# Sample attention of a hybrid decoder step: key blocks outermost over the four pairs, and a second bank for the turned probabilities

## The reference, cut to what matters

```python
s_c = jnp.einsum('bqgrd,bngd->bqgrn', qi, kc) * scale      # compressed keys
p_c = _masked_softmax(s_c, m_c, (-1,))
o_c = jnp.einsum('bqgrn,bngd->bqgrd', p_c.astype(vc.dtype), vc)
imp = ...                     # importance of each 64-key block, from p_c
_, idx = lax.top_k(score, n_top)
s_s = jnp.einsum('bqgrd,bqgksd->bqgrks', qi, k_sel) * scale   # selected blocks
p_s = _masked_softmax(s_s, m_s, (-2, -1))
o_s = jnp.einsum('bqgrks,bqgksd->bqgrd', p_s.astype(v_sel.dtype), v_sel)
s_w = jnp.einsum('bqgrd,bkgd->bqgrk', qi, k_w) * scale        # last 512 keys
p_w = _masked_softmax(s_w, m_w, (-1,))
o_w = jnp.einsum('bqgrk,bkgd->bqgrd', p_w.astype(v_w.dtype), v_w)
return gt[..., 0:1] * o_c + gt[..., 1:2] * o_s + gt[..., 2:3] * o_w
```

## Time and profile before

| | us |
|---|---|
| median of three runs (3066.73 to 3068.82) | 3068.81 |
| the profiled execution | 3069.89 |
| its span, first to last instruction | 3068.1 |
| PE busy in the span | 2789.7 (91%) |
| PE weight loads busy | 2557.5 (83%) |
| DVE busy | 1432.9 (47%) |
| ACT busy | 491.3 (16%) |
| POOL busy | 694.5 (23%) |
| mean granted clock of PE | 0.946 |

### The profile page before, as it was taken

How to read it: one execution, slowest core, us unless ns; L and a number is a source line. 1 busy time by engine, 2 the same in 40 slices (tenths; PEclk the granted TensorE clock), 3 DMA queues, 4 the chain that set the end, 5 groups by cost and what they waited for, 6 DMA issues and landing times. The chain is left out here.

```text
span 3068.1 us, 38688 instructions
## 1 busy us (share of the span) xinstructions
PE 2789.7 (91%) x15429; PEld 2557.5 (83%) x15429; DVE 1432.9 (47%) x2224; ACT 491.3 (16%) x710; POOL 694.5 (23%) x366
## 2 busy tenths in 40 slices
PE   8978786778898899999999998969899999999995
PEld 8978744445558899999999997969799999999983
DVE  4999025555643563333333335854653333333334
ACT  3011123123331220000000002031320000000002
POOL 3431002000002132233232221322133223223210
PEclk9987877699999999999999999979999999999998
DMA  4114541000003011111111111111011111111101
GB/s 152 56 34 140 122 138 41 1 1 1 1 1 114 28 42 41 41 41 45 51 42 44 45 41 28 42 35 42 21 49 41 48 41 41 48 41 41 45 10 59
DMA packets 82854, 145.01 MB, mean 47 GB/s; under 512 B 26382, under 2 KB 54286, under 8 KB 82446
## 3 DMA queue, kind: packets, MB, share of 16 engines
q1 hardware_dynamic: 60126, 129.68, 13.2%
q10 hardware_dynamic: 22640, 14.16, 1.6%
HBM read 134.88 MB, written 13.07 MB: 48 GB/s over the span
## 5 line engine op out<-in xcount | busy, mean ns | idle before, releaser
L580 PE MATMUL PS<-XH,WH 128*128 128x364 f32 x3048 | 682.5, 332 | 65.0 <-ACTq L1027 16.3
L580 PE MATMUL PS<-XL,WH 128*128 128x364 f32 x3048 | 678.5, 331 | 0.0
L580 PE MATMUL PS<-XH,WL 128*128 128x364 f32 x3048 | 678.2, 331 | 0.0
L535 POOL CAST WH<-RAW 128x1024 fp32r<-128x1024 f32 x177 | 207.4, 1172 | 2003.9 <-PE PS L580 1331.0
L580 PEld LDWEIGHTS PS<-XH,WH 128*128 128x128 f32 x3048 | 536.2, 190 | 67.9 <-issue 41.8
L580 PEld LDWEIGHTS PS<-XL,WH 128*128 128x128 f32 x3048 | 535.8, 190 | 0.0
L580 PEld LDWEIGHTS PS<-XH,WL 128*128 128x128 f32 x3048 | 535.3, 190 | 0.0
L537 POOL TENSOR_TENSOR WL<-RAW,WH 128x1024 fp32r<-128x1024 f32 x177 | 466.9, 2638 | 14.2
L561 PE MATMUL PS<-HH,WH 128*128 128x364 f32 x1056 | 354.1, 335 | 29.3 <-DVE Y L1794 15.1
L1794 DVE TENSOR_TENSOR Y<-Y,PS 128x364 f32<-128x364 f32 x480 | 254.0, 533 | 230.9 <-PE PS L566 225.9
L566 PE MATMUL PS<-HL,WH 128*128 128x364 f32 x1056 | 348.2, 330 | 0.0
(11 more groups left out here) (276 smaller groups left out, 2501.5 us busy)
## 6 DMA issues: line engine op xcount, KB each, us to landing
RAW<-wst SPq DMA_DIRECT2D x174, 512.0 KB, 3.3
KVP<-cache SPq DMA_DIRECT2D x64, 128.0 KB, 2.2
XRAW<-xT SPq DMA_DIRECT2D x8, 546.0 KB, 10.5
Y<-xT SPq DMA_DIRECT2D x8, 546.0 KB, 7.4
yT<-Y ACTq DMA_DIRECT2D x3, 1456.0 KB, 9.7
PG<-cache SPq DMA_DIRECT2D x64, 64.0 KB, 2.3
PG<-cache ACTq DMA_DIRECT2D x64, 64.0 KB, 2.3
win_old<-win_past SPq DMA_DIRECT2D x1, 4032.0 KB, 15.9
```

The source lines that it names most:

```text
L535: pool.tensor_copy(WH[:, s, :], RAW[:, s, :]).then_inc(hi_done, 1)
L580: mm = pe.matmul(PS[:, 3 * bank_set + c, 0:CH], w, x[:, k, c * CH:(c + 1) * CH], start=(q == 0 and w is hi and x is XH), stop=(q == len(ks ...
```

## The change

Four loops over the pairs are turned inside out. `L754` and `L760` get loops of their own behind those of `L753` and `L758`. `L758` runs over the halves outside and the pairs inside. `L787` and `L800` run over key blocks outside and pairs inside, with `L789` and `L802` in loops of their own behind them. `S_TURN = (6, 0)` names two banks: even turns go to bank 6, odd ones to bank 0, and PE waits before a turn only until the turn before the last has been moved. ACT's `move` reads from the bank of its turn.

```diff
--- before.py
+++ after.py
@@ -75,6 +75,7 @@
 N_W = AT_F1 + N_FFN
 POOL_ORDER = [6, 7, 4, 5, 2, 3, 0, 1]
 RING = 3
+S_TURN = (6, 0)
 CONV_STEPS = 3
 EARLY = 21
 assert N_W % RING == 0 and EARLY % RING == 0
@@ -751,12 +752,14 @@
                 pe.wait_ge(sp_loaded[b2], 18 * 16 * (gi // 2 + 1))
                 for bb, g, rows, feat, q, at in pairs():
                     pe.matmul(PS[rows, 0, :], q, KWS[b2][feat, bb, :], start=True, stop=True)
+                for bb, g, rows, feat, q, at in pairs():
                     mm = pe.matmul(PS[rows, 1, 0:SS], q, kv("kw")[feat, at:at + SS], start=True, stop=True)
                 mm.then_inc(s_win, 1)
-                for bb, g, rows, feat, q, at in pairs():
-                    for h in range(2):
+                for h in range(2):
+                    for bb, g, rows, feat, q, at in pairs():
                         pe.matmul(PS[rows, 2 + h, :], q, KVP[b2][feat, 8 * bb + 4 * h:8 * bb + 4 * h + 4, 0, :],
                                   start=True, stop=True)
+                for bb, g, rows, feat, q, at in pairs():
                     mm = pe.matmul(PS[rows, 4, 0:SS], q, kv("ks")[feat, at:at + SS], start=True, stop=True)
                 mm.then_inc(s_sel, 1)
                 pe.wait_ge(s_pc, gi + 1)
@@ -765,10 +768,10 @@
                 def turned_tiles(src, cols):
 
                     nonlocal turn
-                    if turn:
-                        pe.wait_ge(s_turned, turn)
+                    if turn >= 2:
+                        pe.wait_ge(s_turned, turn - 1)
                     for n, (lo, hi) in enumerate(cols):
-                        mm = pe.transpose(PS[0:hi - lo, 6, n * P:(n + 1) * P], src[:, lo:hi], ident)
+                        mm = pe.transpose(PS[0:hi - lo, S_TURN[turn % 2], n * P:(n + 1) * P], src[:, lo:hi], ident)
                     mm.then_inc(s_turn, 1)
                     turn += 1
 
@@ -782,10 +785,11 @@
                 turned_tiles(PB[:, 0, :], [(k * P, k * P + P) for k in range(4)])
                 turned_tiles(PB[:, 0, :], [(W_HIST, W_HIST + SS)])
                 pe.wait_ge(s_turned, turn)
-                for bb, g, rows, feat, q, at in pairs():
-                    for k in range(4):
+                for k in range(4):
+                    for bb, g, rows, feat, q, at in pairs():
                         pe.matmul(PS[rows, 7, HD:2 * HD], PTB[:, 0, k * P + 32 * (2 * bb + g):k * P + 32 * (2 * bb + g) + 32],
                                   VWS[b2][:, bb, k, feat], start=(k == 0), stop=False)
+                for bb, g, rows, feat, q, at in pairs():
                     mm = pe.matmul(PS[rows, 7, HD:2 * HD], PTB[0:SS, 0, 4 * P + 32 * (2 * bb + g):4 * P + 32 * (2 * bb + g) + 32],
                                    VN[:, 1, 2 * gi + bb, feat], start=False, stop=True)
                 mm.then_inc(s_pv, 1)
@@ -794,11 +798,13 @@
                 turned_tiles(PB[:, 1, :], [(k * P, k * P + P) for k in range(4, 8)])
                 turned_tiles(PB[:, 1, :], [(8 * P, 8 * P + SS)])
                 pe.wait_ge(s_turned, turn)
+                for k in range(8):
+                    for bb, g, rows, feat, q, at in pairs():
+                        j = 32 * (2 * bb + g)
+                        pe.matmul(PS[rows, 7, 2 * HD:3 * HD], PTB[:, k // 4, (k % 4) * P + j:(k % 4) * P + j + 32],
+                                  KVP[b2][:, 8 * bb + k, 1, feat], start=(k == 0), stop=False)
                 for bb, g, rows, feat, q, at in pairs():
                     j = 32 * (2 * bb + g)
-                    for k in range(8):
-                        pe.matmul(PS[rows, 7, 2 * HD:3 * HD], PTB[:, k // 4, (k % 4) * P + j:(k % 4) * P + j + 32],
-                                  KVP[b2][:, 8 * bb + k, 1, feat], start=(k == 0), stop=False)
                     mm = pe.matmul(PS[rows, 7, 2 * HD:3 * HD], PTB[0:SS, 0, 4 * P + j:4 * P + j + 32],
                                    VN[:, 0, 2 * gi + bb, feat], start=False, stop=True)
                 mm.then_inc(s_pv, 1)
@@ -1068,8 +1074,8 @@
                 def move(dsts):
                     nonlocal turn
                     act.wait_ge(s_turn, turn + 1)
-                    for dst, src in dsts:
-                        ins = act.activation(dst, src, ACT.Copy)
+                    for dst, rows, n in dsts:
+                        ins = act.activation(dst, PS[0:rows, S_TURN[turn % 2], 0:n], ACT.Copy)
                     ins.then_inc(s_turned, 1)
                     turn += 1
 
@@ -1081,15 +1087,15 @@
                     if kind == 0:
                         if gi:
                             act.wait_ge(s_pv, 3 * gi)
-                        move([(PTB[0:NB, 0, 0:P], PS[0:NB, 6, 0:P])])
+                        move([(PTB[0:NB, 0, 0:P], NB, P)])
                         act.wait_ge(s_pv, 3 * gi + 1)
-                        move([(PTB[:, 0, 0:4 * P], PS[:, 6, 0:4 * P])])
-                        move([(PTB[0:SS, 0, 4 * P:5 * P], PS[0:SS, 6, 0:P])])
+                        move([(PTB[:, 0, 0:4 * P], P, 4 * P)])
+                        move([(PTB[0:SS, 0, 4 * P:5 * P], SS, P)])
                     else:
                         act.wait_ge(s_pv, 3 * gi + 2)
-                        move([(PTB[:, 0, 0:4 * P], PS[:, 6, 0:4 * P])])
-                        move([(PTB[:, 1, 0:4 * P], PS[:, 6, 0:4 * P])])
-                        move([(PTB[0:SS, 0, 4 * P:5 * P], PS[0:SS, 6, 0:P])])
+                        move([(PTB[:, 0, 0:4 * P], P, 4 * P)])
+                        move([(PTB[:, 1, 0:4 * P], P, 4 * P)])
+                        move([(PTB[0:SS, 0, 4 * P:5 * P], SS, P)])
 
 
             def split_high(n):
```

## The result

| | before | after |
|---|---|---|
| median, us | 3067.89 (3066.73 to 3068.82, 4 runs) | 3033.47 (3032.53 to 3037.61, 4 runs) |
| the profiled execution (its span) | 3069.89 (3068.1) | 3037.61 (3035.8) |
| stage, first `L748` of G0 to `L653` (`L749` to `L654` after) | 383.23 to 498.28: 115.05 | 384.65 to 461.35: 76.70 |
| what follows it in the span | 2569.8 | 2574.5 |

The ratio is 0.9891 with a 95% interval of 0.9873 to 0.9908: 34.4 us less, where 34.7 were forecast. Lines of the kernel after are shifted: `L754` and `L756` are the window scores (`L753`, `L754` before), `L760` and `L763` the selected scores (`L758`, `L760`), `L766` the importance (`L763`), `L774` the turns (`L771`), `L790` the window products (`L787`), `L804` and `L808` the selected products (`L800`, `L802`), `L654` the convolution's norm (`L653`); on ACT `L1078` is the move and `L1085` the exponential.

A forecast was written before the change was run, and what follows sets the result against it. PE's order in sample attention (groups G0 to G3) bounds now, loads at G1 and G3 afterwards. G3's loads, scores, exponential, turns, products and tail end at 463.6 against 498.28: 3069.89 - 34.7 = 3035.2 us, range 3027 to 3040.

The forecast's parts named there:

- The end of the stage bounds the rest: Sample attention's end at `L653`, 498.28: time won before it moves the rest of the span as a block.
- The sign that I had named against the forecast: Behind `L653`: if the time there grows, the forecast is wrong at its root; no size given.
- Four records ahead: Scores on PE: each pair's strip takes about four records ahead; `L753` to `L763` takes 5.35 us, gaining some 2.7 a group.
- rivals two: Scores: PE already runs pairs abreast, so G1 and G3 keep 2.7 us each; 3039 us, chance 0.05.
- three: Rival on interleaved products: each change of strip drains the one before, so the kernel gets slower; 3085 us, chance 0.06.
- 5.1 us from the importance to the second exponential, covering the window products: DVE and ACT work after `L763`, untouched at 5.1 us; window products four abreast (0.5 to 1.7 us) end under it.
- Selected products: `L800` four abreast plus `L802`: 2.1 us taken, from the nearest row `L778`; 1.2 to 2.1, high end 7.9.
- rivals one: Value products stay serial because of their 128 rows; scores and turns still gain: 15.8 us won, 3053 us, chance 0.09.
- four: Rival: only the turns gain, 1.0 to 1.4 us a group, 5 us in all; 3064 us, chance 0.04.
- Loads: SP's transfers hold G1 until 406.1 and G3 until 445.45; G2 starts near 424.5; gains in G0 and G2 mostly lost.
- SP is done with G1 at 400.0: SP's queue: it goes on at once to G2's loads, which land 24.8 us later, at 424.8.
- The clock in the stage: PE taken at 1.2 GHz in G1 and G3, `L653` at 463.6; 2.4 GHz throughout would give 458.1, 40.2 us won.

The follow-up runs named there:

- a_again: The kernel after, unchanged, run once more: median 3033.40 us (4 runs), ratio 0.9893 to the kernel before.
- e_chunk4: The kernel after with selected value products in chunks of four key blocks, pair by pair within each chunk: 3043.75 us (one run).
- e_chunk8: The kernel after with all eight key blocks of one pair's selected value products before the next pair's: 3044.10 us (one run).
- e_split: The kernel after with selected scores pair by pair again, the 8 new keys' scores still in their own loop: 3033.97 us (one run).
- e_scores: The kernel before with only the score loops changed as in the diff: 3061.24 us (10 runs), ratio 0.9963.
- b_again: The kernel before, unchanged, run once more: 3081.12 us in its profiled execution; seven others on that chip had a median of 3067.11.
- e_values: The kernel before with only the value-product loops changed as in the diff: 3053.18 us (5 runs), ratio 0.9939.
- e_banks: The kernel before with only the second bank for the turns and its looser wait: 3057.36 us (6 runs), ratio 0.9953.
- e_onebank: The kernel after with turns in one bank, each waiting for the turn before: 3042.32 us (4 runs), ratio 0.9915 to the kernel before.

## Why the prediction held, step by step

- **The total**: 34.7 forecast, 34.4 measured; that they agree so closely is partly luck. The stage lost 38.4 us (38.5 in `a_again`), 3.7 more than forecast. Against that, G0 began 1.4 to 1.8 later than in the one profile that the forecast was read from, and that profiled execution, 3069.89, was 2.0 above the median of 3067.89.
- **The end of the stage bounds the rest**: right. `a_again` wins 38.5 us in the stage, 36.7 of them in the span (G0 began 1.8 later), and the rest differs by 0.03. The sign that I had named against the forecast, a longer time behind `L653`, did appear in the first profile; it comes and goes with the clock in the prompt attention, and five of 14 profiles have it (2574.2 to 2575.6; the others 2568.0 to 2570.1).
- **Four records ahead**: right, and now measured (`e_chunk4`, `e_chunk8`, `e_split`). Scores took 5.30 and 5.45 us in G1 and G2, where 5.35 stood for 1.2 GHz, and 4.3 and 4.8 in G0 and G3, where the clock rose on the way. The gain of "some 2.7 a group" was not G1's: 7.08 less 5.35 is 1.7, and 1.8 was measured. That slip enters G0's end, which the loads hide, and rivals two and three.
- **5.1 us from the importance to the second exponential, covering the window products**: right, 412.04 to 417.16. The products were done at 415.84, and PE then waited 1.37 for ACT.
- **Turns**: 2.80 us at 1.2 GHz (417.21 to 420.01) for 3.0, 2.04 at 2.4 GHz for 2.35.
- **Selected products**: 2.30 us with `L808` at 1.2 GHz and 1.34 at 2.4, for 2.1 and 1.3. `L778` was the right row to stand on; rivals one and three fall with `L804`'s 64 records in 1.93, as two does with `e_scores` and four with the time itself. The Trainium skill, "TensorE: Matmul & The Clock Gate", Part 3 (The mechanism), has a weight load overlap running matmuls only on other rows; `L804`, four strips on the same 128 rows in the time of one, its 64 weight loads within the same 1.93 us, disagrees, and the measurement decides.
- **Loads**: G1 held until 406.1 was right (406.74; 406.27 in `a_again`). G2 at 424.5 and G3 held until 445.45 were not: G2 was held to 426.89, and G3 found its loads there, 0.3 us early. The step that failed is "SP is done with G1 at 400.0": its last load went out at 401.85, 2.3 later than before, so G2's landed 2.1 later. The change did not do that: in `b_again`, the same kernel as before, that load goes out at 402.01. 400.0 was read from one execution, and an early one: in 13 of the 14 profiles the stage began at 384.4 or later, in that one at 383.23. G3's then needed less time from SP (12.66 for the pages, not 13.70). G3 began at 445.26 all the same, for 445.45, now set by G2's length and not by its loads (in `a_again` it waited 0.49 for them). So the loads bound G1 and G2, not G1 and G3.
- **The clock in the stage**: taken as 1.2 GHz throughout G1 and G3; G3 had its turns and products at 2.4 GHz in the profile after, and `L654` came at 461.35, not 463.6. This is the mis-sized term, 2.2 us at the end of the stage.

The experiments missed more than the forecast did, always on the same point: for `e_values`, `e_banks` and `e_onebank` I costed waits and left the clock as it was in one profile. What sets the clock of one execution, and whether the order of the stage decides it or chance, stays open; `b_again` shows that the same order can have either.

## What to carry to other kernels

Where several small matrix products use different column strips, issue them in turn over the strips, so that no strip has more than four records not yet done; a short product of another shape between two long ones costs more than its own time. Before pricing such a gain, follow the queue that loads the next step's data: it took 7 of the 46 us that the stage could have lost. And look at more than one execution before explaining a few microseconds by a wait, since here the clock alone moved the same stage by 8.

## What the runs showed of the hardware

Four strips that share all 128 rows run fully side by side: 64 records in 1.93 us at 1.2 GHz, with 16 to a strip at 0.107. In this kernel PE took four unfinished records a strip: the next pair's first started with the thirteenth of sixteen (`e_chunk8`) and the fifth of eight (`e_chunk4`). A stretch with a higher grant can be followed by one with a lower: the kernel after had 0.74 in the 100 us behind the stage and 0.88 in the next, `a_again` 0.69 and 0.95, and the first came out 4.7 us later.
